# Half of the output weights fetched one head earlier, and half of the first feed-forward block fetched and converted ahead, in a two-block transformer kernel on one core

## What is computed

```python
# l = 0, 1; xl: 512 latent tokens, xc: 256 context tokens (updated in layer 0 only)
hl = adaln(xl, g[0], ml[0], ml[1]); hc = adaln(xc, g[0], mc[0], mc[1])
yl, yc = mixer(hl, hc, w_in[l], w_out[l], ...)     # recurrence (4 heads, 2 directions), attention, Fourier
xl = xl + ml[2] * rms_norm(yl, g[1])
xl = xl + ml[5] * rms_norm(swiglu(adaln(xl, g[2], ml[3], ml[4]), w_ffn_in[l], w_ffn_out[l]), g[3])
# the same for xc in layer 0;   swiglu(h) = (silu(h @ w_i[:, :FF]) * (h @ w_i[:, FF:])) @ w_o
# ml, mc = modulation(c, w_mod[l], b_mod[l]): a product of the condition with a 1024 x 6144 matrix
```

## Time and profile before

| | |
|---|---|
| median of three executions | 3327.33 us (3326.36 to 3330.32) |
| the profiled execution: own time, span of its trace | 3326.51 us, 3325.2 us |
| busy in the span: TensorE, weight loads, VectorE, ScalarE, GpSimd | 91%, 72%, 47%, 30%, 10% |
| out projections begin (us from the span's start) | 1670.1 in layer 0, 2876.6 in layer 1 |
| feed-forwards' first products | 1767.3 in layer 0, 2944.8 in layer 1 |
| fetches of `w_out`: 8 of 2048 KB, of `w_ffn_in`: 44 of 1024 KB | median 9.1 us and 7.4 us to landing |

### The profile page before, as it was taken

The page is one execution under the profiler, slowest core; times in us unless marked ns, Lnnn a source line. Parts: engine busy times, 40 slices in busy tenths (PEclk is TensorE's granted clock), DMA queues, the critical chain, the costliest instruction groups (busy, mean ns, idle before and its releaser), DMA issues.

```text
span 3325.2 us, 44100 instructions
## 1 busy us (share of the span) xinstructions
PE 3019.9 (91%) x18434; PEld 2410.0 (72%) x18434; DVE 1573.1 (47%) x3075; ACT 988.3 (30%) x1912; POOL 318.5 (10%) x594
## 2 busy tenths in 40 slices
PE   7988899999999998788689999999999798699998
PEld 4657688888976566677557888888566587478886
DVE  3122544444443255767854424333625566655444
ACT  2011422223341155243232112111315344232222
POOL 0000000000000000544400000000100144200001
PEclk8999999999999998899799999999999799899999
DMA  5423242122222110222422121222111011122322
GB/s 186 151 91 122 82 122 57 44 72 58 64 89 102 51 32 1 80 77 77 142 88 89 51 72 43 77 64 69 46 45 33 16 33 46 51 89 89 102 88 76
DMA packets 227235, 246.62 MB, mean 74 GB/s; under 512 B 5488, under 2 KB 192988, under 8 KB 225500
## 3 DMA queue, kind: packets, MB, share of 16 engines
q1 hardware_dynamic: 227036, 243.79, 22.9%
HBM read 234.34 MB, written 9.44 MB: 73 GB/s over the span
## 4 chain that ended last, share of the span: by engine, by line
PE 55%; DVE 8%; ACT 4%; issue 2%; DMA 1%; POOL 1%; DVEq 0%; SPq 0%; ACTq 0%; POOLq 0%
PE PS L1934 52%; PE PS L1938 2%; PE PS L2143 2%; ACT AR L174 1%; DVE AR L2662 1%; DVE AR L2653 1%; ACT L169 1%; DVE AR L2898 1%; DMA WR<-in_w_ffn_in 0%; DVE STAT L2834 0%; ACT WC L174 0%; DVE EX L2885 0%; ACT EX L174 0%; DVE AR L2671 0%; DMA WR<-in_w_in 0%
## 5 line engine op out<-in xcount | busy, mean ns | idle before, releaser
L1934 PE MATMUL PS<-HI,WC 128*128 128x512 f32 (+3 forms) x2144 | 573.3, 354 | 11.9 <-DVE WC L2879 7.8
L1934 PE MATMUL PS<-WR,HT 128*128 128x256 f32 (+2 forms) x2256 | 513.6, 386 | 15.8 <-ACT AR L174 5.5
L1934 PEld LDWEIGHTS PS<-WR,HT 128*128 128x128 f32 x2256 | 379.8, 198 | 125.8 <-issue 75.9
L1934 PEld LDWEIGHTS PS<-HI,WC 128*128 128x128 f32 x2144 | 383.1, 191 | 69.5 <-DVE WC L2879 9.4
L1934 PE MATMUL PS<-AR 128*64 128x64 f32 (+8 forms) x3756 | 322.3, 271 | 72.9 <-ACT AR L174 18.6
L1934 PE MATMUL PS<-LO,WC 128*128 128x512 f32 (+3 forms) x1072 | 380.0, 355 | 0.0
L1934 PE MATMUL PS<-HT,WR 128*128 128x256 f32 (+3 forms) x1136 | 356.4, 468 | 22.4 <-DMA WR<-in_w_in 6.3
L1934 PEld LDWEIGHTS PS<-AR 128*64 128x64 f32 (+5 forms) x3756 | 278.3, 175 | 124.4 <-issue 49.4
L174 ACT ACTIVATE AR<-PS 128x384 f32<-128x384 f32 (+4 forms) x383 | 164.8, 454 | 683.1 <-PE PS L1934 540.0
L1934 PE MATMUL PS<-DW,DH 128*128 128x384 f32 (+1 forms) x1344 | 357.1, 348 | 0.9 <-DVE AR L2517 0.9
L2879 DVE TENSOR_TENSOR WC<-WR,WC 128x1024 fp32r<-128x1024 f32 x132 | 161.6, 1225 | 382.9 <-ACT WC L174 382.9
(11 more groups left out here) (287 smaller groups left out, 3422.4 us busy)
## 6 DMA issues: line engine op xcount, KB each, us to landing
WR<-in_w_ffn_in SPq DMA_DIRECT2D x44, 1024.0 KB, 7.4
WR<-in_w_in_b SPq DMA_DIRECT2D x51, 512.0 KB, 5.8
WR<-in_w_mod SPq DMA_DIRECT2D x12, 2048.0 KB, 8.1
WR<-in_w_mod SPq DMA_DIRECT2D x24, 1024.0 KB, 5.4
WR<-in_w_ffn_out SPq DMA_DIRECT2D x22, 1024.0 KB, 4.9
WR<-in_w_in SPq DMA_DIRECT2D x40, 512.0 KB, 4.2
WR<-in_w_out SPq DMA_DIRECT2D x8, 2048.0 KB, 9.1
WR<-in_w_in_a SPq DMA_DIRECT2D x8, 1024.0 KB, 5.3
```

The costliest lines, as they stand in the source:

```text
L1934: mm = lambda o, l, r, start, stop: e.o.matmul(o, l, r, start=start, stop=stop, skip_group_check=True)
```

## The change

1. In the fourth head's steps (`first_half`) the first half of the output weights is fetched into slot 1 as soon as head 2 is recorded as ended; the second half goes to slot 0 at the old place. (Before, the halves went to slots 0 and 1, both at the old place.) The modulation's scratch moves from slot 1 to AR.
2. A new raw place "f" of 2048 columns takes rows 0 to 511 of up block 0, fetched right behind the reload of X and XC. Rows 512 to 1023 go to slot 0 at the last tile. The quarters 0 and 1 of block 0 are converted from "f", the quarters 2 and 3 from slot 0. Quarter 0 is converted at the last tile but one.
3. The ring `wcr` has a fourth entry, WD, at its head. It stays for the whole feed-forward.
4. A DMA scratch is made smaller, which gives AR the room.

```diff
+        WC0_AT = 24576
+        wslots["f"] = AR[:, WC0_AT + 2048:WC0_AT + 4096]
...
+        def out_half(wout, c, slot):
+            return load(wout[:, 512 * c:512 * c + 512], 8, 512, slot)
...
-            mods = modulation(1, [XC[:, 1536:1664], WR[:, 7936:8192], AR[:, early.at:early.at + 128]], 7, ["q2"] * 24, width=256, more=freed) if both else iter(())
+            mods = modulation(1, [XC[:, 1536:1664], AR[:, WC0_AT + 512:WC0_AT + 768], AR[:, early.at:early.at + 128]], 7, ["q2"] * 24, width=256, more=freed) if both else iter(())
+            W = []
+
+            def first_half(steps, W=W, l=l, set_until=set_until, heads=heads):
+
+                for n, _ in enumerate(steps):
+                    if heads[2].ended and not W:
+                        wuntil[1] = set_until[2]
+                        W.append(out_half(A["w_out_2"][l], 0, 1))
+                    yield
             for h in range(4):
-                together(with_some(with_some(main(h), mods, MODS[h]), flow, FLOW[l]), preps[h], RATE[l][h], 1)
+                lead = main(h) if h < 3 else first_half(main(h))
+                together(with_some(with_some(lead, mods, MODS[h]), flow, FLOW[l]), preps[h], RATE[l][h], 1)
             carried_end()
             for _ in mods:
                 pass
             join_slot()
-            wuntil[1] = (*set_until[2], ("mod_t", P.count["mod_t"]))
-            W = out_weights(A["w_out_2"][l])
+            W.append(out_half(A["w_out_2"][l], 1, 0))
...
-            wcr = Ring(*[WC[:, 2048 * i:2048 * i + 2048] for i in range(3)])
+            wcr = Ring(at(f"WD{l}", AR_AT + 4 * WC0_AT, 2048, F32R), *[WC[:, 2048 * i:2048 * i + 2048] for i in range(3)])
...
+            def up_rows(r0, r1):
+                return [(0, 256, wi[r0:r1, 0:256]), (256, 256, wi[r0:r1, FF:FF + 256])]
+            first_up = load(up_rows(0, 512), 4, 512, "f")
+
             def stage_w(kind, b):
-                if kind == "up":
+                if kind == "up" and b == 0:
+                    staged["up"] = load(up_rows(512, 1024), 4, 512, 0)
+                elif kind == "up":
...
             def convert(kind, b, c):
-                w = staged[kind]
-                src = w.view[:, 2 * c:2 * c + 2, :] if kind == "up" else w.view[:, :, 512 * c:512 * c + 512]
+                w, k0 = staged.get(kind), 0
+                if kind == "up" and b == 0:
+                    w, k0 = (first_up, 0) if c < 2 else (w, 4)
+                src = w.view[:, 2 * c - k0:2 * c - k0 + 2, :] if kind == "up" else w.view[:, :, 512 * c:512 * c + 512]
...
+                if w is first_up and c == 1:
+                    wuntil["f"] = (("cv_d", n),)
...
+                if i == nt - 2:
+                    convert("up", 0, 0)
                 if i == nt - 1:
                     for j, p in enumerate((ps[0], ps[1], ps[1])):
-                        wcr.until[j] = (("pj", p.n),)
+                        wcr.until[1 + j] = (("pj", p.n),)
                     stage_w("up", 0)
                     stage_w("down", 0)
-                    convert("up", 0, 0)
...
-    nc = _bacc.Bacc("TRN2", target_bir_lowering=False, num_devices=1)
+    nc = _bacc.Bacc("TRN2", target_bir_lowering=False, num_devices=1, dynamic_dma_scratch_size=1024)
```

## The result

The changed kernel takes **3307.46 us** (median of four executions, 3305.35 to 3311.11) beside 3328.41 us (3326.36 to 3330.32) for the kernel before on the same chip. The ratio is 0.9940, 95% interval 0.9924 to 0.9955: 21 us faster, between 15 and 25. Forecast were 13.0 us and a range from 3309 to 3322 us, so the sign was right and the size was not: the time lies 1.5 us outside the range.

What follows compares the result with a forecast made beforehand. TensorE was taken to bound the kernel, fetches costing time only at a few places. Terms 5.4 + 4.0 + 1.0 + 2.6 = 13.0 us took the median from 3327.3 to 3314.3 us, range 3309 to 3322.

Steps and rivals of the forecast that it cites:

- The out projection: Layer 0's out projection: output weights fetched early, products begin right behind the turns; 5.4 us won (4.6 to 6.2).
- The fourth entry: Layer 0's feed-forward: fourth ring entry removes nine waits of 0.29 us, those of 0.75 us stay; 2.6 us won.
- Layer 1's opening: Layer 1's feed-forward opening: second up quarter 2.6 us earlier, less 1.6 us for the clock; 1.0 us won.
- a half clock: Layer 1's feed-forward opening: TensorE's clock falls behind the stop that stays, costing 1.6 us; in layer 0 taken as 0.
- Layer 0's opening: Layer 0's feed-forward opening: `rs` and its chain start earlier, so the second up quarter does; 4.0 us won.
- What bounds the kernel: Over half of the chain is TensorE, DMA about 1%, so a fetch costs time only at a few places.
- The modulation: The early 2 MB fetch among `w_mod` fetches: cost 0, 3.3 us of cover; growing `w_mod` waits would refute it.
- rival 2: Layer 0's feed-forward: all drains' waits go as DVE is relieved; 6.7 us more, 19.7 in all, 3307.6 us; chance 9%.
- Rivals 1: Both openings run half their way at 1.2 GHz, fourth entry only shifts waits; 8.0 us won; chance 19% with 5.
- 3: The early fetch makes two modulation products wait for a whole fetch; 2.6 us won, 3324.7 us; chance 9%.
- 4: In the fourth head six `w_mod` fetches come late; 18 us net lost, 3345.5 us; chance 4%.
- 5: Layer 0's out projection stop has another cause than its fetch; 5.4 us stay, 7.6 won; chance 19% with Rivals 1.

Runs made afterwards that it cites:

- e1: The changed kernel run again without any edit: 3306.74 us, ratio 0.9928 to the kernel before.
- e8: The kernel before with the output weights fetched early, and the raw slots of up and down blocks exchanged: 3322.22 us, ratio 0.9979.
- e2: The kernel before with only the smaller DMA scratch: 3329.49 us, ratio 0.9998.
- e4: The kernel before with only the change's second part, the feed-forward's opening, and a ring of three: 3319.49 us, ratio 0.9966.
- e5: The kernel before with only the ring's fourth entry, placed at its end: 3323.15 us, ratio 0.9981.
- e6: The changed kernel with the ring back at three entries: 3312.80 us, ratio 0.9951 to the kernel before.
- e9: The changed kernel with each block's conversion ahead of its first silu, and a ring of three: 3320.45 us, ratio 0.9971 to the kernel before.
- e10: The changed kernel with the first conversion back at the last tile instead of a tile earlier: 3308.21 us, ratio 0.9935 to the kernel before.
- e7: The changed kernel with each block's conversion recorded ahead of its first silu: 3292.61 us, ratio 0.9895 to the kernel before.
- part 1 alone: The kernel before with only the output weights fetched early and the modulation's scratch moved: 3333.98 us, ratio 1.0012.

## Why the prediction was right about the way and wrong about the size

The fetches and waits were named rightly, and the steps that failed are sizes, all of them too low: 13.0 us in the sum, 20.7 us in the ledger. The out projection gave 2.6 us more: its first products were priced as in layer 1, and the products behind the next stop were put at nothing. The fourth entry gave 2.4 us more or above, since its waits were priced by the printed idle time. Layer 1's opening gave 2.2 us more, 1.6 of them for a half clock that didn't come. Layer 0's opening gave 0.6 us more, since `rs` started earlier than reckoned. One after the other:

**What bounds the kernel, right.** The fetches named in the chain were the causes. The output products began behind the turns, and the first up quarter behind the last output product, as the text said they would. Only in layer 1 it began 0.45 us behind, held by a split on VectorE, where within 0.1 us was expected.

**The out projection: 5.4 us forecast, 8.0 measured.** The first half's start moved as reckoned, but the products then took 1675.06 - 1668.19 = 6.87 us and not the 7.77 us of layer 1. The ends given for this were 4.6 and 6.2; the low one was a repeat of the 8.62 us, the high one (7.0 us) was what came, and the turns overlap the products, so it is 6.5. That is so in seven of the nine executions with the early fetch; in e1 and e8 the stretch is 9.11 and 9.26 us, so 5.0 and 4.8 us are won. The other 1.5 us have no step in the text at all. The four products behind the next stop ran at full clock, 3.60 - 1.98 = 1.6 us shorter. I had used these rows only to say that a short stop may cost 1.6 us or nothing, not asked which of the two this place would do once the stop ahead of it was gone. The profiled executions suggest an answer: where the first half still stopped 4.5 us for its fetch (before, e2, e4, e5) these products took 3.50 to 3.66 us all four times; where it did not, 1.98 or 1.99 us seven times, and 2.45 (e6) and 3.51 us (e9). What decides between them stays open.

**The modulation, right in the main.** The release came 4 us ahead of the next `w_mod` fetch. The last `w_mod` fetch took 5.72 us beside 5.18, and TensorE's waits for these fetches from 1610 us on were three, 4.2 us in all, beside three of 3.5 us before. The prediction named growing waits as a sign of being wrong. Over the executions they are 3.4 to 4.0 us without the early fetch and 3.4 to 5.7 us with it, so a cost of a fraction of a us is not shut out. At the first landmark it can't be told from the scatter. The rule of the Trainium skill's page "DMA: Bandwidth & Descriptors" (Queues, rings and completion order), that descriptors queued behind others wait for them, shows at another place, where it harms nothing. In the list of DMAs, the fetches into "f", queued behind 2 MB of `w_out` and the reload, and the same size alone in the queue:

```profile
AR<-in_w_ffn_in SPq DMA_DIRECT2D x4, 512.0 KB, 12.2
WR<-in_w_ffn_in SPq DMA_DIRECT2D x4, 512.0 KB, 4.6
```

**The opening, layer 0: 4.0 us forecast, 4.6 measured.** From the last output product's printed end to the second quarter 8.66 us were reckoned and 8.12 came. The chain was right, and the clock held across the remaining stops. But the text let ScalarE's `rs` start at that end, and it starts 0.63 us ahead of it (1757.62 beside 1758.25), with the whole chain behind it.

**The opening, layer 1: 1.0 us forecast, 3.2 measured.** The step that failed is the 1.6 us taken for a half clock. A row of stretches over this place (us, busy per engine, PEclk) shows before:

```profile
2942.00:2948.00 6.00, 3.24 (x10) 3.24 (x11) 3.92 (x6) 2.71 (x7) 0.00 (x0) 0.60 0.51 175
```

and after:

```profile
2936.00:2942.00 6.00, 5.67 (x39) 5.44 (x36) 5.58 (x8) 3.12 (x4) 0.00 (x0) 1.00 0.01 5
```

The remaining time is broken by the turns, as in layer 0, into stops of 1.84 and 0.33 us, and behind these the clock stayed at 2.4 GHz. The rule weighed here, from "TensorE: Matmul & The Clock Gate" (HAM oscillation) in the Trainium skill, that gaps between bursts bring the half clock back, was read as making both openings pay; in the changed kernel neither did. The page's own case is one of long waits between short bursts. The trace agrees with it behind the stop of 3.80 us before (the 0.60 above); it doesn't say which of the short stops pay, and neither do these runs, since layer 1 of e10 did pay. The other 0.5 us over the 2.6 us reckoned without the clock are again the start of `rs`, 0.63 us ahead of the last product's printed end (2928.12 beside 2928.75). The half clock of before is no large part of them: VectorE's conversion there ended at 2950.73 + 1.23 = 2951.96, only 0.3 us ahead of the second quarter.

**The fourth entry: 2.6 us forecast, 5.0 to 6.6 measured.** The mechanism was right in each link: the 0.29 us waits went, the 0.75 us ones stayed, for the reason given. The price was wrong, since it took the idle time in the brackets for the cost of the stop, and the upper end of the sum took the same 2.6 us. By the blocks' length such a stop costs 0.5 us, nearly twice what is printed, and there are ten or so. The text had said that blocks shrinking by other than 0.3 us would show it wrong, and they shrank by 0.5 us.

**The rivals.** The time is rival 2's (3307.6), but not by its mechanism: nine waits of 6.7 us remain. Its price was too low as well: with all but two of the waits gone, e7 stands at 3292.6 us. Rivals 1, 3, 4 and 5 did not come.

**What the text did not see at all** is that part 1 alone loses time. It says that slot 0 now holds the half used last, and asks only whether the 1 MB fetch is covered; what the whole up block would pay for this, 6.7 and 6.9 us more of idle time in the two layers, was never priced, so it took the parts as independent. They are not: part 1 alone is 3.9 us slower, part 2 alone 10.6 us faster, both 17.0.

## What to carry to other kernels

Price a short recurring stop by the period of its loop or by the start-to-start time of the products around it, never by the idle time in the brackets alone. When two transfers change slots, ask of each slot who reads it last and which fetch comes next into it; a change that frees one slot early can hold the next fetch at the other. And where a drain waits behind a conversion, first try the order of the two, with a buffer more so that the earlier one need not wait: that was worth 20.2 us here (e7 beside e6, each against its kernel before), where all the fetches gave 17.0 us (e6).

## What the runs showed of the hardware

A single 128x512 product is shown 0.39 us long, while such products start 8.63 / 36 = 0.24 us apart. So the printed idle time begins about 0.15 us later than the time at which the next product could have started. The ends are modelled, and this would account for part of the 0.2 us (ring) and 0.6 us (silu) that the brackets leave out at each stop. More lies inside the groups: from the first of the 24 products behind the 0.75 us stop to the product that follows them it is 2047.74 - 2041.45 = 6.29 us, where 24 in the undisturbed half take 24 x 0.24 = 5.8. These look like small waits for VectorE's next drains. The stopped product starts 0.06 us behind the end of the drain that it waits for (2041.45 beside 2040.71 + 0.68 = 2041.39), and three products inside the group start 0.05 to 0.06 us behind the ends of the next three drains (2042.98, 2044.52 and 2046.23 beside 2042.93, 2044.46 and 2046.18). No row names these waits.
